# Constant products in TensorE's waits, one root for two norms, and two projections by seven products for eight

## What is computed

```python
def first_block(x, c, ctx, ...):                   # two layers
    for l in range(2):
        sh1, sc1, g1, sh2, sc2, g2 = silu(c) @ w_mod[l] + b_mod[l]
        hl = rmsnorm(xl, norm1_g[l]) * (1 + sc1) + sh1
        if l == 0:  # RG-LRU heads and Hyena channels (long convolutions by FFT;
                    # filters = sin(f*(sin(f*(z @ w1 + b1)) @ w2 + b2)) @ w3 + b3)
            yl = concat(y_a, z) @ w_out
        else:       # conformer convolution
            u = (hl @ cf_w1 + cf_b1) -> gate -> depthwise convolution
            yl = silu(layernorm(u)) @ cf_w2 + cf_b2
        xl = xl + g1 * yl
        h = rmsnorm(xl, norm2_g[l]) * (1 + sc2) + sh2
        probs = softmax(h @ router[l]); gates, idx = top_k(probs, 64)  # each expert: its top 64
        xl = xl + g2 * scatter_add(idx, (silu(xs @ w1) * (xs @ w3)) @ w2 * gates)
    return rmsnorm(xl, final_g)
def second_block(x, ...):
    h = rmsnorm(x, norm_gain)            # of the first block's normed result
    proj = h @ w_in                      # 7 kinds of inputs, of four mixers
    mixed = sum(sigmoid(merge_i) * (y_i @ w_branch[i]) for i in range(4))
    return rmsnorm(x + mixed @ w_out, final_gain)
```

## Time and profile before

| | |
|---|---|
| runs | 2486.54, 2488.76 (median), 2493.47 us |
| profiled execution | 2494.18 us, of which 2492.9 us span |
| TensorE busy with products (PE) | 2325.1 us, 93% of the span, 12892 instructions |
| TensorE weight loads (PEld, beside the products) | 1139.9 us |
| VectorE (DVE) | 902.2 us, 36% |
| ScalarE (ACT) | 499.8 us, 20% |
| granted clock of TensorE, mean | 0.975 |

### The profile page before, as it was taken

The page is one execution under the profiler, slowest core; times in us unless marked ns, Lnnn a source line. Parts: engine busy times, 40 slices in busy tenths (PEclk is TensorE's granted clock), DMA queues, the critical chain, the costliest instruction groups (busy, mean ns, idle before and its releaser), DMA issues.

```text
span 2492.9 us, 30364 instructions
## 1 busy us (share of the span) xinstructions
PE 2325.1 (93%) x12892; PEld 1139.9 (46%) x12892; DVE 902.2 (36%) x1601; ACT 499.8 (20%) x887; POOL 0.2 (0%) x4
## 2 busy tenths in 40 slices
PE   6999999799999998989799999988999999999698
PEld 1354345444444433434444444435885447644443
DVE  4548652311111114662211111125762445324452
ACT  1357100211111112021211111121112321113500
POOL 0000000000000000000000000000000000000000
PEclk9999999899999999999899999999999999999899
DMA  7613424499999993645599999952221221122152
GB/s 279 219 34 101 152 96 183 199 421 421 421 421 421 421 419 136 227 170 202 225 421 421 421 421 421 421 236 86 79 83 68 85 64 41 40 82 78 46 177 76
DMA packets 97012, 556.99 MB, mean 223 GB/s; under 512 B 13578, under 2 KB 14090, under 8 KB 40364
## 3 DMA queue, kind: packets, MB, share of 16 engines
q1 hardware_dynamic: 90432, 538.77, 54.9%
q10 hardware_dynamic: 6444, 16.28, 1.7%
HBM read 544.52 MB, written 10.49 MB: 223 GB/s over the span
## 4 chain that ended last, share of the span: by engine, by line
PE 81%; DVE 11%; ACT 3%; DMA 3%; issue 2%; ACTq 0%; SPq 0%; DVEq 0%
PE bank L214 80%; DMA fast_w<-in_w_in 2%; PE bank L217 2%; DVE residual L1457 1%; DMA wmod<-in_w_mod 1%; DVE wring L1362 0%; DVE squares L1423 0%; DVE max L1361 0%; ACT scores_t L2899 0%; ACT squares L1417 0%; DVE fast_s L1814 0%; DVE fast_s L1811 0%; DVE fast_s L1813 0%; DVE fast_s L1812 0%; DVE cf_y L1658 0%
## 5 line engine op out<-in xcount | busy, mean ns | idle before, releaser
L214 PE MATMUL bank<-normed,wring 128*128 128x512 f32 (+2 forms) x1488 | 628.6, 607 | 4.9 <-ACT normed L1631 2.1
L214 PE MATMUL bank<-experts,wring 128*64 128x512 f32 x1792 | 394.8, 595 | 4.2 <-ACT wring L1397 4.2
L214 PEld LDWEIGHTS bank<-normed,wring 128*128 128x128 f32 (+2 forms) x1488 | 247.3, 183 | 312.8 <-issue 304.2
L1423 DVE TENSOR_TENSOR squares<-squares,bank 128x512 f32<-128x512 f32 x32 | 22.0, 688 | 652.6 <-ACT squares L1417 652.6
L214 PEld LDWEIGHTS bank<-experts,wring 128*64 128x64 f32 x1792 | 127.6, 137 | 254.9 <-issue 250.4
L214 PE MATMUL bank<-experts,hs_t 128*64 128x512 f32 x896 | 209.4, 594 | 1.5 <-ACT hs_t L1438 1.5
L214 PE MATMUL bank<-give_t,y 128*128 128x512 f32 x256 | 128.6, 621 | 10.2 <-DVE residual L1457 5.9
L214 PE MATMUL bank<-pick,h_tm 128*128 128x128 f32 x1024 | 123.6, 281 | 2.4 <-DVE pick L1374 2.4
L214 PEld LDWEIGHTS bank<-experts,hs_t 128*64 128x64 f32 x896 | 67.3, 137 | 123.3 <-issue 119.9
L214 PEld LDWEIGHTS bank<-pick,h_tm 128*128 128x128 f32 x1024 | 120.9, 198 | 2.6 <-issue 2.6
L1457 DVE SCALAR_TENSOR_TENSOR residual<-bank,mods,residual 128x512 f32<-128x512 f32 x128 | 96.1, 751 | 69.6 <-PE bank L214 63.9
(11 more groups left out here) (514 smaller groups left out, 2266.1 us busy)
## 6 DMA issues: line engine op xcount, KB each, us to landing
experts<-in_exp_w SPq DMA_DIRECT2D x336, 1024.0 KB, 18.1
normed<-in_exp_w SPq DMA_DIRECT2D x48, 1024.0 KB, 18.8
wring<-in_w_in SPq DMA_DIRECT2D x52, 512.0 KB, 3.7
wmod<-in_w_mod SPq DMA_DIRECT2D x16, 1024.0 KB, 7.8
residual<-in_w_mod SPq DMA_DIRECT2D x16, 1024.0 KB, 5.8
cf_wmod<-in_w_mod SPq DMA_DIRECT2D x16, 1024.0 KB, 5.7
fast_w<-in_w_in SPq DMA_DIRECT2D x30, 512.0 KB, 4.4
wring<-in_cf_w SPq DMA_DIRECT2D x24, 512.0 KB, 3.5
```

The source lines that it names most:

```text
L214: return self.nc.tensor.matmul(out, lhsT, rhs, start=start, stop=stop, skip_group_check=True)
L1423: k.vec(v.tensor_tensor(m.hs[:, e, :], m.hs[:, e, :], k.bank[3 - 2 * e][:, :], ALU.mult), f"{m.name}.hs{i}.{e}")
```

## The change

**Constant products.** A new `warm_tensor(k, b, n, left, right)` puts n products of constants (32 output partitions; 512 columns unless `right` is narrower; without inputs named, ones and a constant table; near the start, zeros) in a bank that nobody reads. They are put: four before the wait for the condition, after a wait for the clearing of the memory that they read; five before the wait for the first sine; four before the filter's products; three of 384 columns between the norm sums of the context and those of x, behind a wait for the first filter parts; three in the first output projection after the twelve first half-products, before the wait for hy1.out3; in both routers one before the softmax, ten before the ranks, one before the first gather; three before and one after the spread c0; one before and one after the spread cn.

**One root for two norms.** With r = 1/sqrt(m + eps), the second norm's factor over the first is 1/sqrt(S), where S is the mean of (final_g^2 + eps) X^2 plus eps^2. So one set of squares is summed with two sets of weights (`two_weights_vector`, `two_sums_tensor`: 16 columns of ones, 16 of final_g^2 + eps), one addition with the constants eps and eps^2, one root and one reciprocal yield both, in strips apart. ScalarE squares each chunk once, TensorE sums once. The small projection is made from the raw residual, with w_small scaled by final_g norm_gain_2 beforehand (on VectorE, before the last scatter), and its result is scaled afterwards; the scaling of X by n1 stands behind the first product of pair 0 (`small_vector`). The load of w_small, 0.4 MB, is issued behind the experts' units.

**Pairs.** The scheme of `fast_tensor` is written as general functions (`Pairs`, `pairs_sync`, `pairs_tensor`, `pair_scalar`, `pair_weights_vector`, `pair_inputs_vector`, `pair_vector`) and used for c2 and w3: four pairs each, the first plain, three by seven block products. In the conformer the addition of the bias to the residual is one instruction for all eight chunks instead of eight, and the weights of units 8 to 12 of the ring are loaded after the layer instead of during it, because the pairs' buffers take their place.

```diff
+def warm_tensor(k, b, n, left=None, right=None):
+    left = k.con("ones", 0, 32) if left is None else left
+    right = k.con("reset") if right is None else right
+    for _ in range(n):
+        k.mm(k.bank[b][0:32, 0:right.shape[1]], left, right)
...
+def pairs_sync(k, f, name, sources, free):
+    for i in range(len(sources) // 2):
+        k.nc.sync.wait_ge(*k.at(f"{name}.d{i - 2}" if i >= 2 else free[i]))
+        for e in range(2):
+            k.nc.sync.dma_start(f.w[i % 2][:, e, :, :], sources[2 * i + e]).then_inc(*k.up(f"{name}{i % 2}{e}", f"{name}.w{i}.{e}", 16))
+        yield
...
+def pairs_tensor(k, f, name, x, n_pairs, behind, ready=None):
+    t = k.nc.tensor
+    def product(dst, w, y, start=True):
+        for c in range(4):
+            ins = k.mm(dst, w[:, c, :], y[:, c, :], start and c == 0, c == 3)
+        return ins
+    for i in range(n_pairs):
+        a, b = (k.bank[n] for n in f.banks[i % 2])
+        w0, w1 = f.w[i % 2][:, 0, :, :], f.w[i % 2][:, 1, :, :]
+        s1, s2, s3, s4 = (f.s[:, i % 2, n, :, :] for n in range(4))
+        t1, t2, t3, t4 = (f.t[:, n, :, :] for n in range(4))
...
+        if i == 0:
+            for c in range(KD):
+                if ready:
+                    t.wait_ge(*k.at(f"{ready}{c}"))
+                ins = k.mm(a[:, :], w0[:, c, :], x[:, c, :], c == 0, c == KD - 1)
+            ins.then_inc(*k.up("tensor", f"{name}.first"))
+            for c in range(KD):
+                ins = k.mm(b[:, :], w1[:, c, :], x[:, c, :], c == 0, c == KD - 1)
+            ins.then_inc(*k.up("tensor", f"{name}.d0"))
+        else:
+            if i >= 2:
+                t.wait_ge(*k.at(f"{name}.out{2 * i - 3}"))
+            product(a[:, LOW], w0[:, 0:4, :], x[:, 0:4, LOW])
+            t.wait_ge(*k.at(f"{name}.s{i}"))
+            product(a[:, UPPER], s2, t2, False).then_inc(*k.up("tensor", f"{name}.a{i}"))
+            product(b[:, LOW], s1, t1)
+            product(b[:, UPPER], s3, t3, False).then_inc(*k.up("tensor", f"{name}.b{i}"))
+            t.wait_ge(*k.at(f"{name}.u{i}"))
+            product(a[:, LOW], w0[:, 4:8, :], x[:, 4:8, LOW], False).then_inc(*k.up("tensor", f"{name}.c{i}"))
+            t.wait_ge(*k.at(f"{name}.c22.{i}"))
+            product(b[:, LOW], s4, x[:, 4:8, UPPER], False)
+            product(b[:, UPPER], w1[:, 4:8, :], t4, False).then_inc(*k.up("tensor", f"{name}.d{i}"))
+        behind(i)
...
+def pair_weights_vector(k, f, name, i):
+    v = k.nc.vector
+    w0, w1, s = f.w[i % 2][:, 0, :, :], f.w[i % 2][:, 1, :, :], f.s[:, i % 2, :, :, :]
+    for e in range(2):
+        v.wait_ge(*k.at(f"{name}.w{i}.{e}"))
+    k.vec(v.tensor_tensor(s[:, 0, :, :], w1[:, 0:4, :], w1[:, 4:8, :], ALU.add))
+    k.vec(v.tensor_tensor(s[:, 1, :, :], s[:, 0, :, :], w0[:, 0:4, :], ALU.subtract))
+    k.vec(v.tensor_tensor(s[:, 2, :, :], w0[:, 0:4, :], w1[:, 0:4, :], ALU.subtract))
+    k.vec(v.tensor_tensor(s[:, 3, :, :], w0[:, 4:8, :], s[:, 1, :, :], ALU.subtract), f"{name}.s{i}")
...
+def pair_vector(k, f, name, i, gate, last):
+    v = k.nc.vector
+    a, b = (k.bank[n] for n in f.banks[i % 2])
+    x0, x1, u = k.X[:, 2 * i, :], k.X[:, 2 * i + 1, :], f.u[:, 0, :]
+    def add(x, y, e, done=None):
+        g = gate(2 * i + e)
+        if g is None:
+            k.vec(v.tensor_tensor(x, y, x, ALU.add), done)
+        else:
+            k.vec(v.scalar_tensor_tensor(out=x, in0=y, scalar=g, in1=x, op0=ALU.mult, op1=ALU.add), done)
+    if i == 0:
+        v.wait_ge(*k.at(f"{name}.first"))
+        add(x0, a[:, :], 0, f"{name}.out0")
+        v.wait_ge(*k.at(f"{name}.d0"))
+        add(x1, b[:, :], 1, f"{name}.out1")
+        return
+    v.wait_ge(*k.at(f"{name}.p{i}"))
+    k.vec(v.tensor_tensor(u, f.u[:, 1 + i % 2, :], a[:, UPPER], ALU.add), f"{name}.u{i}")
+    add(x0[:, UPPER], u, 0)
+    add(x1[:, LOW], u, 1)
+    add(x1[:, UPPER], u, 1)
+    if not last:
+        pair_weights_vector(k, f, name, i + 1)
+    v.wait_ge(*k.at(f"{name}.b{i}"))
+    add(x1[:, UPPER], b[:, UPPER], 1)
+    add(x1[:, UPPER], b[:, LOW], 1, f"{name}.c22.{i}")
+    v.wait_ge(*k.at(f"{name}.c{i}"))
+    add(x0[:, LOW], a[:, LOW], 0)
+    v.wait_ge(*k.at(f"{name}.d{i}"))
+    add(x0[:, UPPER], b[:, LOW], 0, f"{name}.out{2 * i}")
+    add(x1[:, LOW], b[:, UPPER], 1, f"{name}.out{2 * i + 1}")
...
     t.wait_ge(*k.at("sp.w2"))
+    warm_tensor(k, 3, 5, zeros[:, 0:32], zeros)
     t.wait_ge(*k.at("sp.sin0"))
     k.mm(bank[1][0:FHID, :], f.w12[:, 1, :], f.hid[0:FHID, 0, :]).then_inc(*k.up("tensor", "sp.pre1"))
     yield
+    warm_tensor(k, 3, 4, zeros[:, 0:32], zeros)
     yield from taps_tensor(k, f, 0)
     t.wait_ge(*k.at("consts"))
     t.wait_ge(*k.at("sp.row0"))
     yield from rms_tensor(k, "rc", KD, TC, 6)
+    t.wait_ge(*k.at("sp.parts0.1"))
+    warm_tensor(k, 0, 3, right=k.C[:, 0:COFF["signs"]])
     yield from rms_tensor(k, "rx", KD, T, 7)
     t.wait_ge(*k.at("sp.folded"))
...
         out_half_tensor(k, m, i, 0)
+    t.wait_ge(*k.at("consts.more"))
+    warm_tensor(k, 7, 3)
     t.wait_ge(*k.at(f"hy1.out{KR - 1}"))
...
+    t.wait_ge(*k.at("lru.clear"))
+    zeros = m.gw[:, 0:4, :].rearrange("p n c -> p (n c)")
+    warm_tensor(k, 3, 4, zeros[:, 0:32], zeros)
     t.wait_ge(*k.at("cond"))
...
     tokens_tensor(k, m, 0)
+    warm_tensor(k, 0, 1)
     t.wait_ge(*k.at(f"{name}.softmax"))
     for n in range(NT):
         ins = k.turn(bank[2][0:NE, n * P:(n + 1) * P], m.pb[:, n, :])
     ins.then_inc(*k.up("tensor", f"{name}.probs"))
     for n in range(1, NT):
         tokens_tensor(k, m, n)
+    warm_tensor(k, 0, 10)
     t.wait_ge(*k.at(f"{name}.ranks"))
     for n in range(NT):
         ins = k.turn(bank[3][:, n * NE:(n + 1) * NE], m.wk[:, 0, n * P:(n + 1) * P], NE)
     ins.then_inc(*k.up("tensor", f"{name}.slots"))
     t.wait_ge(*k.at(f"{name}.ht{NT - 1}.1"))
+    warm_tensor(k, 0, 1)
...
+    if ahead:
+        ahead()
     scatter_vector(k, m, NPAIR - 1)
...
-    blocks = project_steps(k, "c2", [k.blocks("cf_w2", c) for c in range(KD)], (f"c1.mm{2 * KD - 2}", f"c1.mm{2 * KD - 1}"))
-    next(blocks)
+    blocks = pairs_sync(k, m.fast, "c2", [k.blocks("cf_w2", c) for c in range(KD)], (f"c1.mm{2 * KD - 1}", f"ad.row{NEARLY + 13}"))
     next(blocks)
     all_steps(rows)
     router_sync(k, experts)
     k.nc.sync.wait_ge(*k.at(f"ad.row{NEARLY + 7}"))
     for n in range(2, 8):
         unit_sync(k, experts, n)
-    for n in (8, 9, 10, 11, 12, 0):
-        next(blocks)
-        k.nc.sync.wait_ge(*k.at(f"ad.row{NEARLY + n if n else len(ROWS) - 1}"))
+    next(blocks)
+    k.nc.sync.wait_ge(*k.at(f"ad.row{len(ROWS) - 1}"))
+    for n in range(2):
         unit_sync(k, experts, n)
-    unit_sync(k, experts, 1)
+    all_steps(blocks)
...
+    warm_tensor(k, 6, 3)
     spread_tensor(k, "c0", 2)
+    warm_tensor(k, 6, 1)
     rows = adaln_tensor(k, m.wm, k.cs, NEARLY, len(ROWS), m.rows)
...
+    warm_tensor(k, 0, 1)
     spread_tensor(k, "cn", 7)
+    warm_tensor(k, 0, 1)
     next(rows)
...
-    for i in range(KD):
-        x = k.X[:, i, :]
-        k.vec(v.tensor_scalar(x, x, k.SM[:, i:i + 1], None, ALU.add))
-        v.wait_ge(*k.at(f"c2.mm{i}"))
-        k.vec(v.scalar_tensor_tensor(out=x, in0=k.bank[i % 2][:, :], scalar=k.MOD[:, 1, 16 + i, 0:1], in1=x,
-                                     op0=ALU.mult, op1=ALU.add), f"c2.out{i}")
+    k.vec(v.tensor_tensor(k.X[:, :, :], k.X[:, :, :], k.SM[:, 0:8].unsqueeze(2).broadcast_to([P, KD, T]), ALU.add))
+    v.wait_ge(*k.at(f"cf.ready{KD - 1}"))
+    v.wait_ge(*k.at(f"ad.row{len(ROWS) - 1}"))
+    pair_inputs_vector(k, m.fast, k.H)
+    pair_weights_vector(k, m.fast, "c2", 1)
+    for i in range(KD // 2):
+        pair_vector(k, m.fast, "c2", i, lambda c: k.MOD[:, 1, 16 + c, 0:1], i == KD // 2 - 1)
         if i == 0:
             mods_vector(k, 5)
             router_vector(k, experts)
...
+                t.wait_ge(*k.at(f"n2.out{c}"))
                 ins = k.mm(a[:, :], w0[:, c, :], H[:, c, :], c == 0, c == KD - 1)
...
     k.vec(v.tensor_copy(m.pj[:, 0, :], k.bank[0][:, :]), "w2.c11.0")
+    small_vector(k, m)
...
+    t.wait_ge(*k.at("ws.scaled"))
+    for c in range(KD):
+        if c == 4:
+            spread_tensor(k, "n2", 5, 1)
+        ins = k.mm(bank[6][0:96, :], k.W[:, 0, c, 0:96], k.X[:, c, :], c == 0, c == KD - 1)
+    ins.then_inc(*k.up("tensor", "small.mm"))
     spread_tensor(k, "n1", 4, 0)
...
     fast_tensor(k, m)
...
+def two_weights_vector(k, e):
+    v, g = k.nc.vector, k.SM[:, 16:24]
+    k.vec(v.tensor_tensor(k.GA[:, 3, :], k.vector_of("final_g", 0, 8), k.vector_of("norm_gain_2", 0, 8), ALU.mult))
+    k.vec(v.tensor_tensor(g, k.vector_of("final_g", 0, 8), k.vector_of("final_g", 0, 8), ALU.mult))
+    k.vec(v.tensor_scalar(g, g, EPS, None, ALU.add))
+    k.vec(v.memset(e.rg[:, 0:KD, 0:16], 1.0))
+    k.vec(v.tensor_copy(e.rg[:, 0:KD, 16:32], g.unsqueeze(2).broadcast_to([P, KD, 16])), "n1.weights")
+    v.wait_ge(*k.at("ws"))
+    w = k.W[:, 0, :, 0:96]
```

(15 more changed lines are left out.)

121 lines of the change are left out of this document (70 added, 51 removed).

## The result

The changed kernel takes 2468.6 us (median of 5 runs, 2466.3 to 2473.5), the kernel before 2488.8: the ratio is 0.992, with an interval of 0.9906 to 0.9934. That is 20.1 us faster, where 41.8 were forecast; the time lies above both ranges on record, 2439 to 2455 and 2438 to 2466. In a second set of runs it took 2466.9 (median of 6), ratio 0.9914 (0.9897 to 0.9931). The two profiled executions, 2494.2 and 2467.0, differ by 27.2.

The account below looks back on a forecast made before the run. TensorE was taken as the bound, improved by fewer products, less idling or a faster clock. The terms summed to 42.0 us off the median 2488.8, giving 2447, own range 2439 to 2455; with rivals 1 to 3, 2438 to 2466.

Parts of the forecast that it names:

- rival 4: Constant products count for nothing, added work at 1.2 GHz; gains needing no clock 22.4; 10.7 us slower, 2499.5; chance 0.05.
- Do constants count: Whether constant products on TensorE count for its clock; claimed that they hold 2.4 GHz and raise the clock to it.
- Rivals 1: Constant products hold the clock but do not raise it; the start loses 6.6 us, total 2464; chance 0.13.
- The start: Up to the sums of x: constants raise the clock, nine filter products at full speed, weights earlier; 10.5 us gained.
- The routers: Ten products hidden in each wait for the ranks, gather at 2.4 GHz; gains of 3.5 and 2.2 us.
- First output projection: Three products behind the twelve first half-products, where TensorE had no wait; a loss of 1.5 us.
- clock falls as before: Case at the first output projection: half clock as at 389.8 to 396.6, the three products cost 2.6 us.
- Second layer's front: Constants around the spread at 962 gain 2.9 us; two around the later spread gain 0.5.
- Pairs: Seven block products for eight, some waits for VectorE: 5.1 us in the last projection, 3.5 in the conformer.
- Head: Second block's head, one root for two norms: 13.15 us up to the first large product, 2.1 in sums; 15.3 together.
- Rival 3: The clock falls anyway in idle pieces left before the experts and a row's weights; about 5 us less, 2452; chance 0.05.
- Its signs: Trace marks to expect: fast filter products, short router idle, gather of 7 us, full clock at 459 to 482, head 8.6 us.

Follow-up runs that it names:

- no_constants: The changed kernel without any of the constant products, the waits kept: 2469.05 us, ratio 0.9922 to the kernel before.
- before_again: The kernel before, unchanged, run again for a second profile: 2489.65 us, ratio 0.9997.
- no_start: The changed kernel without the start's thirteen products of zeros and three of 384 columns: 2466.3 us, ratio 0.9903 to the kernel before.
- start_plus: The changed kernel with more constants in two start waits, before the second halves of both filter products: 2460.15 us, ratio 0.9873 to the kernel before.
- best3: The changed kernel with constants moved or added into waits of the start, first output projection, routers and elsewhere, conformer's router set-up later: 2449.35 us.
- ranks13_ng: The changed kernel with 13 constant products instead of ten before the ranks and none before the gather, both routers: 2464.3 us, ratio 0.9894.
- wo_before: The changed kernel with four constant products before the first output projection's first halves instead of three behind them: 2460.5 us, ratio 0.9881.
- after: The changed kernel itself, in its first profiled execution: median 2468.6 us, profiled 2467.0.

## Why the prediction was wrong

- **What bounds the kernel**: right. TensorE at one of two clocks; the edits that need no clock were put at 22.4 in rival 4 and gained 20.7 by the stages (15.3, 3.7, 1.7), 19.4 (15.7 to 23.1) by the runs of no_constants.
- **Do constants count**: right, they hold and raise the clock (2.4 GHz from about 10 us on, behind the first four). Rivals 1 and 4 fell. Transposes did it again, as in the earlier trace rows: here in no_constants, where TensorE does transposes alone in the first of these stretches (24 instructions in 4.45 us, in before_again at 455.8 just so):

```profile
457.90:461.30 3.40, 3.40 (x18) 3.40 (x17) 3.26 (x7) 2.76 (x4) 0.00 (x0) 0.50 1.01 424
...
461.30:464.70 3.40, 0.53 (x5) 0.29 (x3) 3.23 (x9) 1.38 (x2) 0.00 (x0) 1.00 1.01 427
```

  The Trainium skill, "TensorE: Matmul & The Clock Gate", Part 4: PE-mode transpose, says that the full clock does not engage for work in transpose mode, which does not count as busy in the same way; three profiles now speak against it for these float32 transposes (no row says whether they use that mode). It did not matter for the sum: in the changed kernel the clock was up before the transposes.
- **The start (10.5)**: the failing term, and the largest. The step that failed is that all nine filter products would run at full clock (7.7 us) and that what TensorE gains by the sums of x is gained at the end. Only the first half of the filter's products did, at 27.3 in 1.02. Then TensorE came 2.15 us too early for VectorE, and the second half ran at half clock as before: 4.5 gained at the sums. Of these 3.4 were given back to half clock at 94 to 109 and near 332, which no kernel without the constants of the start shows (no_start). Filled waits hold the gain (start_plus, best3); which wait brings which low stretch stays open.
- **The routers (5.7)**: measured 2.0. I let the ten products end at 473.6, 1.6 before the slots. They began 1.5 earlier, since the transposes ahead of them ran faster too, and ended at 472.2; VectorE's ranks came no earlier. So 3.14 us were idle and the clock fell before the gather. This was a gain in front of a fixed end, and it made the wait longer. In both routers the one product before the gather, at half clock, delayed it by 0.6. That this idle piece alone brings the low stretch is not shown (ranks13_ng).
- **First output projection (-1.5)**: right that the three stood where nothing was waited for. They cost 2.7 to 2.9, my own "clock falls as before" (2.6), not the middle of two cases.
- **Second layer's front (3.4 with the later spread)**: 3.3 on average, as forecast.
- **Pairs**: the waits were right (1.06 in the last projection, 1.3 forecast), the products mis-sized: 28 of 256 columns take 12.3 (2437.74 to 2450.02), not 12.0, and the last sums end 2.5 us behind the last product: 3.7 instead of 5.1. In c2 it is 1.7 instead of 3.5: the set-up's wait of 2.8 us was counted (3.1), the half clock behind it (1134.2 to 1137.6, 1.7 us, in four of seven profiles) was not.
- **Head (15.3)**: right in the traces, each of its parts to 0.1 us in seven profiles and more; in the medians of the kernel with this edit alone 11 and 13. The small weights landed at 1653.4, and VectorE had its next step, the last scatter, only at 1660.6.
- **The sum**: a second failure. I carried the gain over from an execution 5.4 above the median, and said so, but priced every low stretch in it as present in each execution. The start without constants ends at 70.0 to 75.8, and the forecast's own 74.4 was near the top. The profiled executions differ by 27.2, the medians by 20.1: of the 7 between them 5.4 were to be foreseen.
- Rival 3 (the clock falls anyway in the idle pieces left) was nearest to what happened, though it named other pieces, and gave it 5 us and a chance of 0.05. The constants fell short by 15.
- **Its signs**: the filter's products at 27.3 in 1.02, full clock at 960 to 970, the 8.6 us of the head and two waits over 1 us in each pair stage came. An idle piece under 2 us before the ranks' transposes, a gather of 7 us and full clock throughout 459 to 482 did not: they are the router's and show the same fault as the start.

## What to carry to other kernels

In this kernel constants on TensorE paid where they filled a wait up to its end and delayed nothing: 19 us for 59 products, most of them so placed, 0 to 3 for the 49 of the change. Before a stage is priced, ask who sets its end; time won on TensorE ahead of a result of VectorE is only a longer wait, as the 3.14 us before the slots. And where the clock falls at other places in each execution, price a stretch by several profiles, not by one.

## What was not expected of the hardware

The same work, from the same program, took 1104.9 us in one profile and 1112.5 in another, and the stretches of half clock lay at other places (in the first 450 us at 62.1 and 389.8, or at 384.6 alone). Products of zeros by zeros raise the clock like any others. And the same wait can have a low stretch behind it or not: 2.81 us in the conformer had one in four of seven profiles, 1.27 us at 100 us in wo_before had none, and 2.3 us near 330 had one in after and none in no_start. Which of the waits is followed by a low stretch was not settled.
